# Two joined transformer blocks on one core: boundaries with added squares and idle products, gate columns in quarters, taps on tiles 2 and 3, the first norm among the modulation units

## The chip, the cores and the metric

One core of one Trainium2 chip runs the whole program. The metric is device time in microseconds of one execution. The kernel before took 2717.93, the median of three runs (2711.74 to 2718.31).

## The reference

For 512 tokens of width 1024, in fp32: two layers of a first block, then a second block (attention with chosen keys, window attention, MLP).

```python
def first_block(x, c, w_ada, b_ada, ...):
    c_act = silu(c)
    for l in range(2):
        mod = c_act @ w_ada[l] + b_ada[l]
        sh_mix, sc_mix, gt_mix, sh_mlp, sc_mlp, gt_mlp = split(mod, 6)
        h = rms_norm(x, g_pre_mix[l]) * (1 + sc_mix) + sh_mix
        y = mixer(h, ...)
        x = x + gt_mix * rms_norm(y, g_post_mix[l])
        h = rms_norm(x, g_pre_mlp[l]) * (1 + sc_mlp) + sh_mlp
        f = square(relu(h @ w_ff1[l])) @ w_ff2[l]
        x = x + gt_mlp * rms_norm(f, g_post_mlp[l])

def mixer(h, ...):
    x_m, z, glu_a, glu_b = split(h @ w_in)
    x_c = silu(causal_depthwise_conv(x_m, w_conv_m, b_conv_m))      # 4 taps
    q, k, v = ...                        # per head of 256, from x_c, x_c, x_m
    gates = concat(q, k, v) @ w_gates + b_gates                     # 8 columns: 4 input, 4 forget
    h_m = sigmoid(z) * group_layer_norm(mlstm_chunkwise(q, k, v, gates), 4)
    a = causal_depthwise_conv(glu_a * sigmoid(glu_b), w_dw, b_dw)   # 31 taps
    a = silu(group_layer_norm(a, 8))
    return concat(h_m, a) @ w_out
```

## The kernel before

A tensor of 512 tokens by 1024 features lies in SBUF as 8 tiles of 128 features by 512 tokens. Each weight product is done in split precision: weights and tiles are each a high and a low fp32r part, and a product of 128x128 weights is three matmuls (L1944 to L1946). Weights come in chunks of 512x256, 24 matmuls' worth, through a ring of four: SP loads a chunk (L598), ScalarE writes its high part (L856), POOL its low part (L774). Every engine works its queue in program order; what side work stands between which chunks is written out by hand in each engine's program.

**Start.** SP loads x, c and the four first modulation units (`load_ada` L614, each 1024x512 of `w_ada`). TensorE transposes x, VectorE copies it to X (L1449). `ada_unit` on VectorE multiplies a unit's eight 128x512 pieces by c and adds them up (L1318, L1321); `ada_columns` (L2017) sums over partitions on TensorE.

**A norm.** `norm_stats`: ScalarE squares eight tiles (L886); `norm_sums` on TensorE adds each over its rows with products against one column of ones, 8 a tile (L1990); ScalarE takes the root (L879), VectorE refines it (L1334 to L1341), TensorE spreads it over partitions (L1997). `normalise` then makes each tile: VectorE product (L1355), ScalarE high half (L896), VectorE low half (L1361). Where a residual is added, the added value comes of L1380, X of L1383, and the squares of X follow tile by tile. For the first norm after a product, POOL already adds the squares (`sum_squares`, L783).

**A layer of the first block.** The gated stage: four pair-chunks of `glu_a` and `glu_b` (L1483 makes the gated tile); in layer 0 the rest of the modulation streams in here, one unit a stage p. Then xm, V, Q, K, the gates, z, the heads, the output product, a boundary, the MLP in four groups, a boundary. The 31-tap convolution of a pair of tiles (`long_conv`, L1424 and L1429) is VectorE's; two tiles (6 and 7 before) have a share of their taps scaled by ScalarE (L942, L952) and added by POOL (`taps.add`, L800). `short_conv` is the 4-tap one, `xm_low` (L1491) and `xc_low` (L1497) low parts of the V, Q and K operands. The gates are 8 output rows of one bank (L2091), with transposes of V between (L2075); VectorE adds the bias, centres the values (L1533) and runs the scans; in the z stage it squares the convolved tiles centred (L1561) on means that TensorE forms (L2116). After the last convolution come the modulation's bias and gains (L1682 to L1689), ahead of the boundary.

## Time and profile before

| | us |
|---|---|
| median of three runs | 2717.93 |
| the profiled execution, on the device | 2711.68 |
| its span in the trace | 2709.8 |
| TensorE busy (PE) | 2543.5, 94% |
| VectorE (DVE) | 1281.1, 47% |
| POOL | 1064.7, 39% |
| ScalarE (ACT) | 967.7, 36% |

The span is all that happens between the first and the last instruction; 1.9 us lie around it. Busy time counts matmuls, arithmetic and copies, not waits. The mean granted clock of TensorE was 0.919 of full speed (1.00 is 2.4 GHz, 0.50 is 1.2 GHz).

### The profile page before, as it was taken

Reading aid. Unit: us, or ns where it says so; the run is one execution under the profiler, and the core shown is the slowest. Engines: PE = TensorE matmul, PEld = TensorE weight load, DVE = VectorE, ACT = ScalarE, POOL = GpSimd, SP = SyncE. Lnnn points to the kernel's source line nnn. Section 1 sums busy time; section 2 is a strip of 40 time slices with the busy share of each in tenths; the row PEclk is TensorE's granted clock in tenths of the full one; section 3 lists DMA queues with packets and bytes.
Section 4 is the critical chain, followed back from the end, with each engine's and each line's share of the span. In section 5 each row is a group of like instructions: output and inputs, shape, how many; then the busy total and the mean of one; then the engine's idle time right before and its main releaser. Section 6 shows DMA issues by size and latency. Waiting matters only on the chain.

```text
span 2709.8 us, 29315 instructions
## 1 busy us (share of the span) xinstructions
PE 2543.5 (94%) x10776; PEld 1980.5 (73%) x10776; DVE 1281.1 (47%) x1998; ACT 967.7 (36%) x1530; POOL 1064.7 (39%) x529
## 2 busy tenths in 40 slices
PE   4988899999999999889989999999999999999998
PEld 3776477778888778647777888876776668788887
DVE  4789934754433569973444112124566323312212
ACT  1337553232222333755233223324533322322322
POOL 1348822424434424882242444442421003444443
...
DMA packets 215166, 239.77 MB, mean 88 GB/s; under 512 B 9690, under 2 KB 188698, under 8 KB 215066
## 3 DMA queue, kind: packets, MB, share of 16 engines
...
q8 instruction: 61, 1.00, 0.2%
...
## 4 chain that ended last, share of the span: by engine, by line
PE 81%; DVE 6%; issue 3%; ACT 2%; POOL 2%; DMA 0%; DVEq 0%; SPq 0%; POOLq 0%; ACTq 0%
PE product L1944 21%; PE product L1945 21%; PE product L1946 21%; PE side L1990 3%; PE side L2367 3%; PE product L2389 2%; PE side L2091 2%; PE side L2377 1%; PE side L2174 1%; PE product L2198 1%; PE side L1997 1%; DVE side L1429 1%; POOL slot_f L800 1%; POOL ring_low L774 1%; PE side L2192 1%
## 5 line engine op out<-in xcount | busy, mean ns | idle before, releaser
L774 POOL TENSOR_TENSOR ring_low<-ring_f,ring_high 128x1024 fp32r<-128x1024 f32 (+1 forms) x350 | 838.8, 2402 | 1475.2 <-ACT ring_high L856 1475.2
L1944 PE MATMUL product<-slot_r,ring_high 128*128 128x512 f32 x2792 | 1126.6, 403 | 74.0 <-POOL ring_low L774 29.1
L1945 PE MATMUL product<-slot_r,ring_low 128*128 128x512 f32 x2792 | 1114.5, 399 | 0.0
L1946 PE MATMUL product<-slot_r,ring_high 128*128 128x512 f32 x2792 | 1113.7, 399 | 0.0
L1944 PEld LDWEIGHTS product<-slot_r,ring_high 128*128 128x128 f32 x2792 | 531.1, 190 | 224.6 <-issue 41.7
L856 ACT ACTIVATE ring_high<-ring_f 128x1024 fp32r<-128x1024 f32 (+1 forms) x350 | 367.7, 1053 | 746.8 <-DMA ring_f<-in_w_ff 333.6
L1946 PEld LDWEIGHTS product<-slot_r,ring_high 128*128 128x128 f32 x2792 | 531.4, 190 | 128.6
L1945 PEld LDWEIGHTS product<-slot_r,ring_low 128*128 128x128 f32 x2792 | 532.0, 191 | 123.7 <-issue 0.5
L1398 DVE SCALAR_TENSOR_TENSOR va<-product,sqt 128x512 f32<-128x512 f32 x96 | 66.3, 691 | 391.1 <-ACT sqt L910 391.0
L1429 DVE SCALAR_TENSOR_TENSOR side<-slot_f,cols,side 128x512 f32<-128x512 f32 x332 | 220.7, 747 | 0.0
L1408 DVE TENSOR_TENSOR slot_f<-product,slot_f 128x512 f32<-128x512 f32 x64 | 44.3, 691 | 226.3 <-PE product L1946 226.3
L910 ACT ACTIVATE sqt<-product 128x512 f32<-128x512 f32 x96 | 57.5, 599 | 194.0 <-PE product L1946 194.0
L1990 PEld LDWEIGHTS side<-ones,slot_f 128*128 128x128 f32 x608 | 104.3, 266 | 20.7 <-ACT slot_f L886 12.3
L1990 PE MATMUL side<-ones,slot_f 128*128 128x1 f32 x608 | 104.3, 303 | 11.4 <-ACT slot_f L886 11.1
L1318 DVE SCALAR_TENSOR_TENSOR side<-slot_f,cact,side 128x512 f32<-128x512 f32 x144 | 108.8, 756 | 7.9 <-DMA slot_f<-in_w_ada 2.1
L800 POOL TENSOR_TENSOR slot_f<-slot_f,sqt 128x512 f32<-128x512 f32 x60 | 87.2, 1467 | 26.7 <-ACT sqt L952 26.7
L1408 DVE TENSOR_TENSOR X<-product,X 128x512 f32<-128x512 f32 x32 | 22.1, 692 | 148.2 <-PE product L1946 148.2
L1390 DVE TENSOR_TENSOR slot_r<-va,slot_r 128x512 fp32r<-128x512 f32 x96 | 87.5, 922 | 0.0
L2367 PE MATMUL side<-slot_f 64*128 64x256 f32 (+3 forms) x128 | 80.5, 732 | 5.0 <-DVE slot_f L1842 3.6
L800 POOL TENSOR_TENSOR slot_f<-slot_f,va 128x512 f32<-128x512 f32 x60 | 81.4, 1374 | 3.0 <-ACT va L952 3.0
L886 ACT ACTIVATE slot_f<-X 128x512 f32<-128x512 f32 x56 | 34.5, 628 | 93.1 <-DVE X L1383 43.4
L2389 PEld LDWEIGHTS product<-slot_f 128*128 128x128 f32 x272 | 64.1, 325 | 1.4 <-DVE slot_f L1850 1.2
...
## 6 DMA issues: line engine op xcount, KB each, us to landing
ring_f<-in_w_ff SPq DMA_DIRECT2D x128, 512.0 KB, 3.7
...
```

The source lines that it names most:

```text
L774: pool.tensor_tensor(ring_low[:, s, :, 0:n], ring_f[:, s, :, 0:n], ring_high[:, s, :, 0:n].bitcast(F32), ALU.subtract).then_inc(low_ready. ...
L800: pool.tensor_tensor(tile(SC, t), tile(SC, t), tap[u % 4], ALU.add).then_inc(tap_used.sem, 1)
L856: act.activation(ring_high[:, s, :, 0:n], ring_f[:, s, :, 0:n], ACT.Copy).then_inc(high_ready.sem, 1)
L1318: ins = dve.scalar_tensor_tensor(ada_acc[:] if b and kk == 3 else PM[0][:], ada_raw(slot, b)[:, kk, :], c_col, PM[0][:], ALU.mult, ALU.add)
L1390: dve.tensor_tensor(tile_r(SD, t), va[:, t % 2, :], tile_r(SC, t).bitcast(F32), ALU.subtract).then_inc(fs_ready.sem, 1)
L1429: ins = dve.scalar_tensor_tensor(sum_out, src(t, k, T), wk, sum_in, ALU.mult, ALU.add)
L1944: pe.matmul(out_ap, high, rhs_high, start=start, stop=False)
L1945: pe.matmul(out_ap, low, rhs_high, start=False, stop=False)
L1946: return pe.matmul(out_ap, high, rhs_low, start=False, stop=stop)
L1990: ins = pe.matmul(sums[:, s:s + 1], squares[:, s * P:(s + 1) * P], ones[:, 0:1], start=start and s == 0, stop=stop and s == BLK - 1)
L2367: pe.matmul(PM[u % 2][:, 0:n], q, (AKD if a else BKD)(kv)[b:b + HD, k0:k0 + n], start=True, stop=True).then_inc(qk_2.sem, 1)
L2389: ins = pe.matmul(bank(o)[:, h * HD:(h + 1) * HD], PT[u % 4][:, s * P:(s + 1) * P], VT[0 if a else 1][:, (k0 + s) * P + kv * HD:(k0 + s) * ...
```

## The change

- **Start.** c and unit 0 are loaded first, then x in four pieces, then units 1, 2 and 3, each to buffers of its own. x's first squares come among the units; its high halves of weights are made after them. Tokens' sums of the first norm stand between the unit columns on TensorE.
- **Gated stage of layer 0.** Half of each later unit's load goes out one pair of chunks earlier.
- **Gates.** The product of each head writes rows of its own, at 32 times the head, and the four run for one weight column group each; a second picking product adds and moves the forget rows.
- **Taps.** The tap shares are tiles 2 and 3 instead of 6 and 7 and begin at chunk 11 instead of 21; ScalarE and POOL do them two a chunk through the gated, xm and later stages. The convolution order of VectorE shifts by a pair.
- **Boundaries.** The squares at residual additions are added on POOL, as at the other norms; TensorE has products with the identity and no use (`keep_busy`) while it waits. Bias and gain operations go to places ahead of the boundary, or behind it. POOL's additions stand before three low parts of the next stage.

```diff
 SHARES = NT - SHARED
+TAP_TILE = 2
 TAPS = (CONV_C - 1) * SHARES
-TAPS_FROM = 21
+TAPS_FROM = 11
...
-            sp.dma_start(x_rows, w["x"][0].rearrange("(s p) d -> p s d", p=P)).then_inc(x_loaded.sem, 16)
-            sp.dma_start(c_rows, w["c"][0].rearrange("(t p) -> t p", p=P)).then_inc(x_loaded.sem, 16)
-            for unit in range(ADA_FIRST):
-                load_ada(0, unit_cols(unit), unit)
+            def load_first(unit):
+                for b in range(2):
+                    src = w["w_ada"][0, b * 4 * P:(b + 1) * 4 * P, unit_cols(unit)]
+                    sp.dma_start(ada_raw(FIRST_RAW[unit], b), rows_of(src)).then_inc(first_loaded[unit].sem, 16)
+            sp.dma_start(c_rows, w["c"][0].rearrange("(t p) -> t p", p=P)).then_inc(c_loaded.sem, 16)
+            load_first(0)
+            for s in range(BLK):
+                sp.dma_start(x_rows[:, s, :], w["x"][0, s * P:(s + 1) * P, :]).then_inc(x_loaded.sem, 16)
+            load_first(1)
...
-                        load_ada(l, unit_cols(ADA_FIRST + p), ADA_FIRST + p)
+                        load_ada(l, unit_cols(ADA_FIRST + p), ADA_FIRST + p, halves=(0,))
+                    load_pair(LAYER, I_GLU + 4 * p + 2, w_in, 0, 2 * D + p * CW, load_params if l and p == 0 else None)
+                    if l == 0:
+                        load_ada(l, unit_cols(ADA_FIRST + p), ADA_FIRST + p, halves=(1,))
...
                 taps = Taps()
-                for i in range(I_GATE):
+                early = 2 if l else 0
+                for i in range(early):
+                    low_part(place, LAYER, i)
+                sum_squares(place, 0)
+                for i in range(early, I_GATE):
...
                         taps.add(place, 2)
-                taps.add(place, 26)
+                taps.add(place, 10)
...
                     low_part(place, LAYER, i)
-                    taps.add(place, 4)
+                    taps.add(place, 2)
...
+                sum_squares(place, 1)
+                sum_squares(place, 2)
...
                         low_part(Place(l, g), LAYER, i)
-                sum_squares(place, 3, 1)
+                sum_squares(place, 3)
...
             low_part(place, SECOND, 0)
+            low_part(place, SECOND, 1)
...
-            for i in range(AHEAD):
-                high_part(Place(), LAYER, i)
+            for t in range(NT):
+                wait(act, Place(), xt_done, t + 1)
+                act.activation(X[:, t, :], PB[t % 4][:], ACT.Copy).then_inc(x_ready.sem, 1)
...
                 norm_stats(place, 0, lambda t: X[:, t, :], lambda t: wait(act, place, x_ready, t + 1))
+                if l == 0:
+                    for i in range(AHEAD):
+                        high_part(place, LAYER, i)
                 split_high(place, 0, lambda t: shift[:, t:t + 1])
+                taps = Taps()
...
                         ahead.of(place, I_GLU + 4 * p + t % 2)
+                        if t == 4:
+                            taps.first(place)
+                        if p > 1 and t % 2 == 0:
+                            taps.make(place, 2)
...
                         act.activation(tile(SC, t), bank(o_glub(t))[:], ACT.Sigmoid).then_inc(taken[o_glub(t) % 4].sem, 1)
+                    if p > 1:
+                        taps.make(place, 2)
                     ahead.of(place, I_GLU + 4 * p + 2)
+                    if p > 1:
+                        taps.make(place, 2)
                     ahead.of(place, I_GLU + 4 * p + 3)
+                    if p > 1:
+                        taps.make(place, 2)
...
-                taps = Taps()
...
                     ahead.of(place, I_XM + t)
+                    if t % 2 == 0:
+                        taps.make(place, 2)
...
-                token_rstd(place, m)
+                if place.layer or m:
+                    token_rstd(place, m)
+                else:
+                    wait(dve, place, r_ready, 1)
...
+                def add_bias(a, b):
+                    steps.wait()
+                    steps.did(dve.tensor_tensor(md[:, a:b], md[:, a:b], cols[:, V_BADA + a:V_BADA + b], ALU.add))
+                    steps.wait()
+                def gate_gain(dst, m, g):
+                    steps.did(dve.tensor_tensor(scale[:, dst * NT:(dst + 1) * NT], md[:, m * NT:(m + 1) * NT],
+                                                cols[:, g:g + NT], ALU.mult))
+                def post_mixer():
+                    gate_gain(1, 2, V_GPOSTM)
+                    steps.did(dve.tensor_copy(shift[:, NT:2 * NT], md[:, 3 * NT:4 * NT]))
+                def pre_hidden():
+                    steps.did(dve.scalar_tensor_tensor(scale[:, 2 * NT:3 * NT], md[:, 4 * NT:5 * NT], 1.0,
+                                                       cols[:, V_GPREF:V_GPREF + NT], ALU.add, ALU.mult))
...
+                if l:
+                    add_bias(16, 48)
+                    post_mixer()
...
-                long_conv(place, 2, 0, 14)
+                long_conv(place, 4, 0, 14)
...
                 ada_take()
+                if l == 0:
+                    add_bias(16, 32)
+                    post_mixer()
                 if l:
-                    long_conv(place, 2, 14, 20)
+                    long_conv(place, 4, 14, 20)
...
                 if l:
-                    long_conv(place, 2, 20, 24)
+                    long_conv(place, 4, 20, 24)
...
                 xm_low(4, 5)
+                xm_low(6, 7)
                 short_conv(place, 6)
-                xm_low(6, 7)
                 xc_low(0, 1, 2, 3)
-                long_conv(place, 2, late, late + 3)
+                long_conv(place, 4, late, late + 3)
                 xc_low(4, 5, 6, 7)
-                long_conv(place, 2, late + 3)
-                long_conv(place, 4, 0, 12 if l == 0 else 22)
+                long_conv(place, 4, late + 3)
+                long_conv(place, 6, 0, 12 if l == 0 else 22)
...
                 wait(dve, place, vtr_done, 8)
-                dve.tensor_scalar(gt, PM[0][0:8, :], bgate, None, ALU.add).then_inc(gates_biased.sem, 1)
...
-                steps.did(dve.scalar_tensor_tensor(glf, PM[1][0:HEADS, :], 0.0, gu, ALU.min, ALU.subtract))
+                steps.did(dve.scalar_tensor_tensor(glf, forget_gates, 0.0, gu, ALU.min, ALU.subtract))
...
+                        pre_hidden()
...
                 ada_take()
-                steps.wait()
-                steps.did(dve.tensor_tensor(md[:, 16:48], md[:, 16:48], cols[:, V_BADA + 16:V_BADA + 48], ALU.add))
-                steps.wait()
-                for dst, m, g in ((1, 2, V_GPOSTM), (3, 5, V_GPOSTF)):
-                    steps.did(dve.tensor_tensor(scale[:, dst * NT:(dst + 1) * NT], md[:, m * NT:(m + 1) * NT],
-                                                cols[:, g:g + NT], ALU.mult))
-                steps.did(dve.scalar_tensor_tensor(scale[:, 2 * NT:3 * NT], md[:, 4 * NT:5 * NT], 1.0,
-                                                   cols[:, V_GPREF:V_GPREF + NT], ALU.add, ALU.mult))
-                steps.did(dve.tensor_copy(shift[:, NT:2 * NT], md[:, 3 * NT:4 * NT]))
...
                 normalise(place, 2, 1, lambda t: scale[:, 2 * NT + t:2 * NT + t + 1], lambda t: shift[:, NT + t:NT + t + 1])
+                if l == 0:
+                    add_bias(40, 48)
+                    gate_gain(3, 5, V_GPOSTF)
...
-            def norm_sums(place, m, chain=None):
-                if chain is not None:
-                    wait(pe, place, sq_sums, (NT - 2) * (chain + 1))
+            def keep_busy(side, n):
+                for _ in range(n):
+                    pe.matmul(side[:], ident[:], ones[:, 0:1].to_broadcast([P, T]), start=True, stop=True)
+            def norm_sums(place, m, updates=False, busy=(0, 0), between=None):
+                side = PM[1] if updates else PM[0]
+                if updates:
+                    for t in range(NT - 1):
+                        wait(pe, place, sq_ready, 8 * m + t + 1)
+                        keep_busy(side, 1)
+                    wait(pe, place, sq_ready, 8 * m + NT)
+                    token_sums(PM[3], square(m, NT - 1), True, False)
+                    wait(pe, place, sq_sums, (NT - 2) * (m + 1))
+                    ins = token_sums(PM[3], square(m, 0), False, True)
+                else:
+                    wait(pe, place, sq_sums, (NT - 2) * (m + 1))
                     token_sums(PM[3], square(m, 0), True, False)
-                for t in range(NT) if chain is None else (NT - 1,):
-                    wait(pe, place, sq_ready, 8 * m + t + 1)
-                    ins = token_sums(PM[3], square(m, t), t == 0, t == NT - 1)
+                    wait(pe, place, sq_ready, 8 * m + NT)
+                    ins = token_sums(PM[3], square(m, NT - 1), False, True)
                 ins.then_inc(sq_summed.sem, 1)
+                keep_busy(side, busy[0])
+                if between is not None:
+                    between()
...
             pe.wait_ge(consts.sem, 1)
-            pe.wait_ge(x_loaded.sem, 32)
+            pe.wait_ge(c_loaded.sem, 16)
...
             for t in range(NT):
+                if t == 0:
+                    pe.wait_ge(x_loaded.sem, 16 * BLK)
...
                 ins.then_inc(xt_done.sem, 1)
-            for k in range(ADA_FIRST):
-                ada_columns(Place(), k)
...
                 place = Place(l)
+                if l == 0:
+                    ada_columns(place, 0)
+                    ada_columns(place, 1)
+                    wait(pe, place, x_ready, 5)
...
                 for r, n in ((0, V_BCN + NT), (1, P), (2, P), (3, (CONV_C - 28) * NT)):
-                    ins = pe.transpose(PM[0][:, r * P:r * P + n], rows[0:n, r, :], ident[0:n, 0:n])
+                    ins = pe.transpose(params_bank(l)[:, r * P:r * P + n], rows[0:n, r, :], ident[0:n, 0:n])
                 ins.then_inc(cols_done.sem, 1)
-                norm_sums(place, 0)
+                if l == 0:
+                    norm_sums(place, 0, between=lambda: ada_columns(place, 2))
+                    ada_columns(place, 3)
+                else:
...
-                                n += 1
-                                if a == len(kinds) - 1 and dt == 1 and hd == HEADS - 1:
-                                    ins.then_inc(done.sem, 1)
-                                if n % 3 == 0:
-                                    value_transposes(n // 3 - 1)
+                                ins = pe.matmul(PM[0][32 * hd:32 * hd + 32, :], weights[:, 2 * a + dt, :], src,
+                                                start=kind == 0 and dt == 0, stop=kind == 2 and dt == 1)
+                            if a == len(kinds) - 1 and dt == 1:
+                                ins.then_inc(done.sem, 1)
+                            for _ in range(2 if kind == 2 else 1):
+                                value_transposes(moved)
+                                moved += 1
...
                     else:
-                        wait(pe, place, tap_used, TAPS - SHARES + t - SHARED + 1)
+                        wait(pe, place, cv_ready, conv_count(t))
...
                     ada_columns(place, ADA_GLU + 3)
-                norm_sums(place, 1, 0)
-                norm_sums(place, 2)
+                norm_sums(place, 1, busy=(2, 0))
+                norm_sums(place, 2, True, (2, 3))
...
             mlp_group(Place(LAYERS, FF - 1), SECOND, J_FF, U_FF, 0)
-            norm_sums(place, 2, 1)
+            norm_sums(place, 2, busy=(2, 2))
```

## Rows read from the trace of the kernel before

**Rows 1.** Page: head, and the costliest groups.
```profile
span 2709.8 us, 29315 instructions
...
PE 2543.5 (94%) x10776; PEld 1980.5 (73%) x10776; DVE 1281.1 (47%) x1998; ACT 967.7 (36%) x1530; POOL 1064.7 (39%) x529
...
L774 POOL TENSOR_TENSOR ring_low<-ring_f,ring_high 128x1024 fp32r<-128x1024 f32 (+1 forms) x350 | 838.8, 2402 | 1475.2 <-ACT ring_high L856 1475.2
...
L800 POOL TENSOR_TENSOR slot_f<-slot_f,sqt 128x512 f32<-128x512 f32 x60 | 87.2, 1467 | 26.7 <-ACT sqt L952 26.7
```
**Rows 2.** Who waited for whom, TensorE: us in total, times, longest.
```profile
PE product L1944 <- POOL ring_low L774: 29.1, 7, 8.9
PE side L2017 <- DVE ada_acc L1318: 27.3, 4, 7.7
```
**Rows 3.** Timeline, VectorE 15:54: start, us, what, count [idle before, releaser].
```profile
24.14 0.75 DVE L1321 TENSOR_SCALAR side<-slot_f,cact 128x512 f32<-128x512 f32 x1 [2.06 <-DMA slot_f<-in_w_ada]
...
32.44 0.75 DVE L1321 TENSOR_SCALAR side<-slot_f,cact 128x512 f32<-128x512 f32 x1 [1.89 <-DMA slot_f<-in_w_ada]
```
**Rows 4.** Timeline, TensorE 46:73.
```profile
52.71 13.81 PE L1990 MATMUL side<-ones,slot_f 128*128 128x1 f32 x64
...
72.47 0.77 PE L1944 MATMUL product<-slot_r,ring_high 128*128 128x512 f32 x1 [2.47 <-DVE slot_r L1361]
```
**Rows 5.** Stretches: length, busy PE, PEld, DVE, ACT, POOL, PEclk, DMA, GB/s.
```profile
5.00:10.00 5.00, 1.21 (x6) 1.22 (x7) 0.00 (x0) 0.88 (x1) 0.00 (x0) 1.00 1.03 408
...
540.00:545.00 5.00, 2.08 (x8) 1.78 (x8) 2.80 (x6) 0.53 (x1) 0.00 (x0) 0.50 0.14 50
...
570.00:575.00 5.00, 5.00 (x23) 4.04 (x22) 4.14 (x6) 3.06 (x4) 0.42 (x1) 1.00 0.09 17
```
**Rows 6.** Timeline of three engines, layer 0's gated stage.
```profile
98.21 0.99 SPq L614 DMA_DIRECT2D slot_f<-in_w_ada  x2
...
104.55 0.75 DVE L1321 TENSOR_SCALAR side<-slot_f,cact 128x512 f32<-128x512 f32 x1 [6.10 <-DMA slot_f<-in_w_ada]
...
186.75 0.77 PE L1944 MATMUL product<-slot_r,ring_high 128*128 128x512 f32 x1 [5.50 <-DVE slot_f L1483]
```
**Rows 7.** Timeline, TensorE: gate products, and 64-row scores in the second block.
```profile
279.04 2.74 PE L2091 MATMUL side<-slot_f,ring_f 128*8 128x512 f32 x6
...
1952.75 0.70 PE L2348 MATMUL side<-slot_f 64*128 64x256 f32 x4
```
**Rows 8.** Timeline, VectorE in layer 0, 228:343.
```profile
228.12 1.53 DVE L1424 TENSOR_SCALAR side<-slot_f,cols,small 128x512 f32<-128x512 f32 x2 [2.83 <-issue]
...
295.52 0.74 DVE L1533 TENSOR_SCALAR slot_f<-side,small 8x512 f32<-8x512 f32 x1 [3.67 <-PE product L2075]
...
336.97 1.29 DVE L1561 SCALAR_TENSOR_TENSOR slot_f<-side,slot_f 128x512 f32<-128x512 f32 x2
...
341.94 0.69 DVE L1561 SCALAR_TENSOR_TENSOR slot_f<-side,slot_f 128x512 f32<-128x512 f32 x1 [3.69 <-PE side L2116]
```
**Rows 9.** Timeline, TensorE in the z stage of both layers.
```profile
316.72 0.80 PE L1944 MATMUL product<-slot_r,ring_high 128*128 128x512 f32 x1 [8.87 <-POOL ring_low L774]
...
1220.99 1.88 PE L2116 MATMUL side<-slot_f,ones 128*128 128x512 f32 x4
```
**Rows 10.** Timeline, the mixer's boundary in layer 0, and layer 0's end.
```profile
530.79 1.29 POOL L783 TENSOR_TENSOR slot_f<-slot_f 128x512 f32<-128x512 f32 x1 [5.18 <-ACT slot_f L886]
...
534.47 2.31 DVE L1685 TENSOR_TENSOR scale<-mod,cols 128x8 f32<-128x8 f32 x2
...
540.38 2.08 PE L1997 MATMUL side<-ident,inv_cols 128*128 128x128 f32 x8 [5.83 <-DVE inv_cols L1341]
...
545.15 13.81 PE L1990 MATMUL side<-ones,slot_f 128*128 128x1 f32 x64 [2.70 <-ACT slot_f L886]
...
564.93 0.76 PE L1944 MATMUL product<-slot_r,ring_high 128*128 128x512 f32 x1 [2.47 <-DVE slot_r L1361]
...
940.30 1.35 PE L1997 MATMUL side<-ident,inv_cols 128*128 128x128 f32 x8 [1.42 <-DVE inv_cols L1341]
```

134 lines of the change are left out of this document (86 added, 48 removed).

## The prediction

> **What bounds the kernel now.** I read, in this order, the page's first block, the list of who waited for whom, then the timeline of every stretch where TensorE stood idle for over 0.7 us. TensorE is busy for 94% of the span [rows 1], and nearly all of that is split-precision products, which the change leaves alone. What can move is the 166 us in which it has no work, and the stretches where it is busy with little (sums over squares, gate rows, slow clock). The longest list of waits says where: POOL's low halves of weights, 29.1 us in 7 waits, and the modulation columns at the start, 27.3 us in 4 [rows 2]. In time order the reader should see five kinds of place. (a) The start: the first product begins at 72.47 [rows 4], with VectorE's modulation units waiting for their DMAs [rows 3]. (b) Layer 0's gated stage, where VectorE is the pace and TensorE waits 5.50 us for it [rows 6]. (c) The gate and z stage of both layers, where POOL is late by 8.87 us and VectorE's convolution ends last [rows 8, 9]. (d) The boundaries where a residual is added and the next norm taken: 13.81 us of one-column sums at the slow clock, and short steps one after another [rows 10]. (e) The end, which is short.
>
> **Part 1, the start: -26 us.** Before, one pair of buffers serves all four units: a unit's VectorE work is 6.4 us (24.14 to 32.44 less the wait of 1.89), and with the wait it is 8.3 [rows 3]. Now each has a slot of its own, c is loaded first, and x lies between units 0 and 1. The queue moved 408 GB/s when kept full [rows 5], 5.1 us for 2.1 MB; with the first bytes at about 2.9, unit 0 has landed at 8, x at 13, unit 1 at 18, and units 2 and 3 ahead of need. VectorE then runs three units without a stop: 18.3 + 3 x 6.4 = 37.5, plus 0.8 for the parameter copies. The 13.81 us of input squares [rows 4] go off the path, six of their eight groups replaced by POOL's additions and the rest done while VectorE works. After the last unit come the rstd refinement (0.9), spread (2.1) and unit 3's columns (8 passes, 1.7, from 64 in 13.81), small copies and bias (1.0), and the 2.5 us that the first normalised tile takes [rows 4]: 46.5. That is 26 earlier. The bounds are 22, if the small parameter DMAs ahead of unit 2 or chunk 2 behind unit 4's first half hold things, and 29, if DMA starts sooner. The weight chunks land by 41 and are covered by the wait for unit 3; without that cover each late chunk costs its own landing time.
>
> **Part 2, layer 0's gated stage: -6.** Unit 5's load is issued at 98.21 and VectorE sits idle 6.10 us until 104.55 [rows 6]. Its first half now goes out one chunk pair earlier, its second one stays; the first half's 3.2 us of work (half of 6.4) fall into the wait, and the second half has less to share the queue with: VectorE is some 5.3 earlier. It is busy without a gap from there to the 5.50 us wait at 186.75, so TensorE's restart comes 5.3 earlier, and with a gap that short perhaps without the slow products after it. Against: the taps of tiles 2 and 3 now start here. ScalarE gets two scalings per chunk, POOL two additions of 1.47 each beside a low part of 2.4 [rows 1]: 5.3 of the 5.6 us that TensorE takes per chunk of 24 products (23 or 24 start in 5 us [rows 5], 0.23 apart in the trace). Hidden, but with 0.3 us to spare. Range -2 to -8.
>
> **Part 3, gate columns.** Before: 24 products into 8 columns, 48 passes of 0.45 us (6 in 2.74 with the last one's tail [rows 7]), 21.4 us a layer, and 8 groups of transposes. After: four heads in four column quarters. From above: they run one after another, nothing gained, plus 0.9 for a second picking product. From below: four at once, 21.4 to 5.4. The nearest row is the pair of 64-row products in different row halves: 4 passes of 256 columns, in a line 0.22 each and 0.89 with no tail, end in 0.70 with the last one's tail in it [rows 7], so they overlap in part. I take a factor of two, -8 us of TensorE.
> The Trainium skill (TensorE: Matmul & The Clock Gate, Part 3) states that three column tiles gave 2.38 times, and that weight loads run ahead beside products only where the row group differs, which speaks against four times here, since all rows are used; no row of this trace shows column tiles. By its 2.38 the term would be an estimated -11 instead of -8, and neither changes what ends last in layer 0.
>
> **Part 4, the z stage: layer 0 -13, layer 1 -23.** POOL's additions are spread over chunks from 11 on, instead of a burst of 26 and then 4 a chunk: the waits of 8.87 (one a layer [rows 9]) and of 3.1 at the fifth z chunk (of the 29.1 [rows 2]) go in both layers. In layer 0 VectorE is next. It waited 3.67 for the gates at 295.52 and then ran to 336.97 without a stop, 41.4 us [rows 8]. With the gate stage shorter by 8 the 3.67 go; the low part of tile 6 moves into the 2.83 idle at 228.12 [rows 8], 2.4; and POOL being less busy, operations with two SBUF inputs wait less for it, here 3 to 7 of the 41 plus those before. So VectorE ends some 10 to 13 earlier, at about 325 on the old scale, and TensorE's third mean, at 341.9 before [rows 8], follows at once: -13 (bounds -4 and -18). Layer 1 has most of this convolution done before, so TensorE is the pace: gates -8, POOL's waits -12, slow products after them -1.5, K stage -2.4, second picking product +0.9: -23 at 1220.99 [rows 9] (bounds -12 and -27).
>
> **Part 5, boundaries: -5.8 twice, -2.6, -2.4.** There are four with added squares. Squares come in pairs, the last 8.2 us after the first; 64 one-column passes take 13.81 [rows 10]. POOL's six additions of 1.29 run behind them and end at 9.4; one pass group of 1.0 and it is done at 10.5: -3.3. The clock is at its lower level (0.50) in such a stretch [rows 5], and one-column sums did not raise it in 13.81 us; a dummy product is two passes of 0.45 [rows 7], 0.9 at 2.4 GHz and 1.8 at 1.2. Seven of these fit in 8.2 us only at the higher level; started low, three of them last 5 us, and products did bring the clock up between 565 and 570, where it is at 1.00 from 570 on [rows 5, 10]. The spread then takes 1.35 rather than 2.08 [rows 10]: -0.7. Two dummies outlast the 1.4 us refinement [rows 10] by 0.4 (by 2.2 if slow), three the tile's 2.5 by 0.2. Update part: -3.4 (-1 to -4.5).
> Ahead of the mixer's boundary the bias and gain operations leave the path, in both layers: 5.83 idle becomes 1.8 to 3.6, and two of those took 2.31 for 8 columns beside POOL [rows 10]. With the spread's 0.7, that is -2.3 to -4.8, middle -3.8. Against it, POOL's three low parts of the next stage now stand behind the sums and are still running when the first normalised tile's low half, an operation with two SBUF inputs, wants to go: +1.4 (0 to 2.3). Together -5.8.
> The Trainium skill (SBUF — State Buffer, who interferes with whom) has this as an exclusive lock for a whole instruction between a GpSimd operation and a VectorE one with two SBUF inputs; the 2.31 us row agrees. By that rule applied to all eight low halves the boundary would lose an estimated 7, but POOL has only three parts to do there, so the sum keeps 1.4.
> At the end of a layer the residual's spread came 1.42 after [rows 10], already short, so the dummies there cost 0.4 to 2.2: -2.6 and -2.4. In the second block's middle norm and last norm there are only dummies: +1.0 each (0 to 3.5).
>
> **The sum.** -26 -6 -13 -23 -5.8 -5.8 -2.6 -2.4 +1 +1 = -82.6. The gate columns are inside part 4. Profiled span 2709.8, execution 2711.7: 2629.1. That execution is the fastest of the runs shown, 6 below their median 2717.9; by the median it would be 2635. I say 2632.
>
> **Rivals.** *A, quarters in a line.* Layer 1 loses the 8, layer 0's VectorE waits for the gates about 5 of it: 13 less, 2645. For it: no row shows column tiles; against: the row halves overlap.
> *B, POOL sets the pace.* The additions from chunk 11 on slip, so that low parts come late in the gated and projection stages. The wait that VectorE shows beside POOL [rows 10] may work the other way round: with 0.4 more on each addition a chunk is 6.1 us against 5.6, and 0.5 on 19 chunks, twice, is 19 us: 2651. Against it: POOL is busy for 39% of the span, and the ring holds four chunks.
> *C, slower than before.* The same mechanism, with ScalarE in it: its scalings wait for POOL's additions, its high halves stand behind them in order, POOL's low halves behind those. It decides the sign once a chunk from 11 to 29 takes over 5.6 + 83/38 = 7.8 us in both layers; at 8.2, 2730. Against it: ScalarE is busy for 36% of the span [rows 1], and there are four tap buffers between the two.
> *D, the start is held by something else* (the PE's order, small DMAs, the slow clock), and gives 14 instead of 26: 2644.
> *E, all goes well*: locks gone, clock up, four quarters at once: 2612.
> *F, dummies at 1.2 GHz everywhere*, so that each of the boundaries loses its gain: 2652.
>
> **Chances.** Forecast (2620 to 2640) 0.40; A 0.14; B 0.10; C 0.04; D 0.12; E 0.11; F 0.06; the change does in part not what it says, ending within 0.3% of before, 0.03. Range for 8 in 10: the unknown bounds summed in squares give about 17 on each side, and A, B, D and F reach to 2655: 2606 to 2660. A measurement here can tell some 0.3% from no change. Faster by over 0.3%: 0.93; within: 0.03; slower: 0.04.
>
> **What would show it.** First product at 46 or so, three modulation units back to back (part 1). Restart in layer 0's stage within 1 us of the need (part 2). Starts of the four quarter products closer than 0.89 us (part 3); no wait for POOL's low halves after the gates, VectorE's convolution ending ahead of a single idle stretch of TensorE in layer 0, none in layer 1 (part 4). Two short sum groups instead of 64 passes, done 10.5 us after the first square, PEclk at 1.0 by the first product, one VectorE low half over 1.5 us (part 5). The prediction is wrong if ring waits appear between chunks 11 and 29, or if VectorE's modulation units still wait for DMAs.

## The result, and the profile after

The changed kernel takes 2626.77 us (median of four, 2624.44 to 2628.85) against 2717.32 for the kernel before (median of four): a ratio of 0.9682, 95% interval 0.9668 to 0.9695, or 91 us less by the medians. The profiled execution is the second fastest of the four, 2624.85, 87 below the profiled one of before. The forecast was 2632, with 8 chances in 10 for 2606 to 2660. Page head and the list of who waited for whom (TensorE; us in total, times, longest) of the changed kernel, where the lines of the weight products are now L2042 to L2044:

```profile
span 2623.1 us, 29172 instructions
...
PE 2502.1 (95%) x10670; PEld 1926.1 (73%) x10670; DVE 1261.5 (48%) x1995; ACT 971.4 (37%) x1538; POOL 1106.6 (42%) x559
```
```profile
PE side L2248 <- DVE slot_f L1633: 14.3, 2, 7.2
...
PE side L2238 <- DVE slot_f L1662: 7.6, 1, 7.6
...
PE product L2042 <- POOL ring_low L804: 4.3, 2, 4.0
```

Against [rows 2] POOL's late low halves fell from 29.1 us to 4.3, and the modulation columns from 27.3 to one wait of 5.7. In their place stand two waits of 7.2 (one a layer) for VectorE's gate bias (L1633), and one of 7.6 for its convolution, in layer 0. TensorE is busy for 41 us less, and idle for 45 less.

Every kernel here has the same 2792 high-part products in the same order, so the n-th of them is a milestone. The start of the same product in both traces, and what lies between:

| up to | before | after | moved | this part | forecast |
|---|---|---|---|---|---|
| first product | 72.47 | 50.59 | -21.9 | -21.9 | -26 |
| restart in layer 0's gated stage | 186.75 | 164.94 | -21.8 | +0.1 | -6 |
| end of layer 0's z stage | 353.40 | 318.20 | -35.2 | -13.4 | -13 |
| last part of layer 0's output product | 507.97 | 471.74 | -36.2 | -1.0 | 0 |
| mixer's boundary, layer 0 | 564.93 | 522.29 | -42.6 | -6.4 | -5.8 |
| layer 0's end | 964.11 | 919.09 | -45.0 | -2.4 | -2.6 |
| z stage of layer 1 | 1276.95 | 1205.26 | -71.7 | -26.7 | -23 |
| heads of layer 1 | 1347.02 | 1272.21 | -74.8 | -3.1 | 0 |
| mixer's boundary, layer 1 | 1444.11 | 1363.42 | -80.7 | -5.9 | -5.8 |
| layer 1's end | 1833.83 | 1749.42 | -84.4 | -3.7 | -2.4 |
| end of the span | 2709.8 | 2623.1 | -86.7 | -2.3 | +2 |

**The start.** Timeline of VectorE, POOL and TensorE (start us, us, what, count [idle before, releaser]):

```profile
9.72 0.75 DVE L1377 TENSOR_SCALAR side<-slot_f,cact 128x512 f32<-128x512 f32 x1 [6.91 <-DMA slot_f<-in_w_ada]
...
20.37 0.75 DVE L1377 TENSOR_SCALAR side<-slot_f,cact 128x512 f32<-128x512 f32 x1 [4.30 <-DMA slot_f<-in_w_ada]
...
27.42 0.75 DVE L1377 TENSOR_SCALAR side<-slot_f,cact 128x512 f32<-128x512 f32 x1 [0.63 <-DMA slot_f<-in_w_ada]
...
45.68 2.34 POOL L804 TENSOR_TENSOR ring_low<-ring_f,ring_high 128x1024 fp32r<-128x1024 f32 x1 [5.44 <-ACT ring_high L893]
...
45.90 2.13 DVE L1538 SCALAR_TENSOR_TENSOR scale<-mod,cols 128x8 f32<-128x8 f32 x1
...
50.59 0.76 PE L2042 MATMUL product<-slot_r,ring_high 128*128 128x512 f32 x1 [5.36 <-DVE slot_r L1420]
```

VectorE starts unit 1 at 20.37 and unit 2 at 27.42, as they land: with x, 8.4 MB since the first bytes at about 2.9, 342 GB/s on average. The rate was not that all along. In three stretches of 4 us (length, busy PE, PEld, DVE, ACT, POOL, PEclk, DMA share, GB/s):

```profile
14.00:18.00 4.00, 3.23 (x15) 3.23 (x16) 2.00 (x3) 1.56 (x3) 0.00 (x0) 1.00 1.05 387
18.00:22.00 4.00, 3.13 (x27) 3.04 (x25) 1.56 (x3) 3.74 (x8) 0.00 (x0) 1.00 1.07 311
22.00:26.00 4.00, 0.00 (x0) 0.00 (x0) 3.79 (x6) 3.98 (x8) 3.46 (x3) 0.93 1.04 384
```

The dip to 311 has as high a DMA share as its neighbours; in it run the small parameter loads that SP issues between units 1 and 2, some 400 packets of 512 bytes. Later an operation on 8 columns takes 2.13 us while POOL works on a low part.

**The gated stage.** VectorE, POOL, TensorE:

```profile
83.79 2.34 DVE L1374 SCALAR_TENSOR_TENSOR side<-slot_f,cact,side 128x512 f32<-128x512 f32 x3 [3.78 <-DMA slot_f<-in_w_ada]
...
113.15 2.46 DVE L1488 SCALAR_TENSOR_TENSOR side<-slot_f,cols 128x512 f32<-128x512 f32 x2
...
113.31 3.45 POOL L830 TENSOR_TENSOR slot_f<-slot_f,va 128x512 f32<-128x512 f32 x2
...
164.94 0.77 PE L2042 MATMUL product<-slot_r,ring_high 128*128 128x512 f32 x1 [6.63 <-DVE slot_f L1574]
```

The wait of 5.50 [rows 6] is still there, as 6.63. Unit 5's second half lands after VectorE has used the first, and an operation that took 1.42 us for its pair before takes 2.46 beside POOL's tap additions, once for each of two pairs.

**Gates and z stage, layer 0**, TensorE:

```profile
241.38 1.07 PE L2213 MATMUL side<-slot_f,ring_f 128*32 128x512 f32 x8
...
265.44 1.87 PE L2248 MATMUL side<-slot_f,ident_sums 128*4 128x512 f32 x2 [7.22 <-DVE slot_f L1633]
...
302.71 3.75 PE L2238 MATMUL side<-slot_f,ones 128*128 128x512 f32 x4 [7.60 <-DVE slot_f L1662]
```

Eight passes into four quarters take 1.07 us, last tail and all, where six into 8 columns took 2.74 [rows 7]. Behind them TensorE waits twice for VectorE.

**A boundary**, layer 0's mixer (TensorE, and VectorE's refinement). The sums begin 8.5 us after the first square is done (at 503.5) and end in 2.43 (64 passes in 13.81 [rows 10]). The two idle products at 514.35 (four passes) run until 518.1; the spread waits for them and starts at 517.91, 2.1 us past the refinement's end:

```profile
503.56 7.01 PE L2102 MATMUL side<-ones,ident 128*128 128x512 f32 x12 [2.70 <-ACT slot_f L923]
...
512.06 2.43 PE L2088 MATMUL side<-ones,slot_f 128*128 128x1 f32 x16
...
514.35 3.76 PE L2102 MATMUL side<-ones,ident 128*128 128x512 f32 x4
...
515.69 0.16 DVE L1397 SCALAR_TENSOR_TENSOR inv_cols<-side,inv_cols 128x4 f32<-128x4 f32 x1
...
517.91 1.92 PE L2095 MATMUL side<-ident,inv_cols 128*128 128x128 f32 x8
```

### The profile page after: what moved, and what is told of

It reads as the page before. It is cut to its first block, busy times and chain, and to the rows that moved or that the text cites. A ratio compares the mean times of both kernels' runs of the same rounds, so it can differ in the third digit from the quotient of the medians.

```text
span 2623.1 us, 29172 instructions
## 1 busy us (share of the span) xinstructions
PE 2502.1 (95%) x10670; PEld 1926.1 (73%) x10670; DVE 1261.5 (48%) x1995; ACT 971.4 (37%) x1538; POOL 1106.6 (42%) x559
## 4 chain that ended last, share of the span: by engine, by line
PE 81%; DVE 11%; ACT 1%; issue 1%; POOL 1%; DVEq 0%; POOLq 0%; ACTq 0%
PE product L2042 22%; PE product L2044 22%; PE product L2043 22%; DVE side L1488 5%; PE side L2490 3%; PE product L2512 2%; PE side L2500 1%; PE side L2297 1%; PE product L2321 1%; PE side L2088 1%; PE side L2095 1%; PE side L2102 1%; DVE slot_r L1589 1%; PE side L2315 1%; POOL slot_f L813 1%
## 5 line engine op out<-in xcount | busy, mean ns | idle before, releaser
L2042 PE MATMUL product<-slot_r,ring_high 128*128 128x512 f32 x2792 | 1120.1, 401 | 39.1 <-DVE slot_r L1420 9.3
L2044 PE MATMUL product<-slot_r,ring_high 128*128 128x512 f32 x2792 | 1107.1, 397 | 0.0
L2042 PEld LDWEIGHTS product<-slot_r,ring_high 128*128 128x128 f32 x2792 | 527.4, 189 | 190.4 <-issue 35.3
L2044 PEld LDWEIGHTS product<-slot_r,ring_high 128*128 128x128 f32 x2792 | 527.1, 189 | 126.3
L813 POOL TENSOR_TENSOR slot_f<-slot_f 128x512 f32<-128x512 f32 x66 | 84.5, 1280 | 95.9 <-ACT slot_f L923 89.4
L830 POOL TENSOR_TENSOR slot_f<-slot_f,va 128x512 f32<-128x512 f32 x60 | 88.5, 1494 | 2.7 <-ACT va L989 2.4
L830 POOL TENSOR_TENSOR slot_f<-slot_f,sqt 128x512 f32<-128x512 f32 x60 | 81.5, 1379 | 16.1 <-ACT sqt L989 16.1
L2102 PE MATMUL side<-ones,ident 128*128 128x512 f32 x130 | 74.7, 712 | 12.9 <-ACT slot_f L923 12.9
```

The costliest lines, as they stand in the source:

```text
L813: pool.tensor_tensor(square(m, 0), square(m, 0), square(m, t), ALU.add).then_inc(sq_sums.sem, 1)
L830: pool.tensor_tensor(tile(SC, t), tile(SC, t), tap[u % 4], ALU.add).then_inc(tap_used.sem, 1)
L2042: pe.matmul(out_ap, high, rhs_high, start=start, stop=False)
L2044: return pe.matmul(out_ap, high, rhs_low, start=False, stop=stop)
L2102: pe.matmul(side[:], ident[:], ones[:, 0:1].to_broadcast([P, T]), start=True, stop=True)
```

## Experiments

Each is the changed kernel with the edit shown. Medians are of four runs; ratios are to the kernel before on the same chip, where the changed kernel has 0.9682 (0.9668 to 0.9695). A per cent of the ratio is 27 us, so the intervals are some 4 to 7 us to either side. Where a number of microseconds is said to come of the medians, it is the run's median less 2626.77; the kernel before took 2712.7 to 2714.6 on the chips of these runs and 2717.3 on that of the result, so such a number can be off by some 3 to 5 us, and the ratios go before it. Single places are compared by the milestones. They agree to 0.5 us at the first product where an edit leaves it alone. Further on they step without any edit there. Between the milestones at 318 and 425 us of the changed kernel its own profiled execution had the clock at 1.00 nearly throughout, and eight of the eleven others lost up to 6 us there with no more than 0.6 us more of idle time: with x first (e9), the first 12 us of that stretch had a mean granted clock of 0.80, and 5.9 us are lost in all. In the second block five of the profiled executions lost 3.5 to 4.4 us in the same way. So behind layer 0's z stage a difference of under some 6 us between two milestones tells little, unless the place itself shows the wait.

No run takes back the added squares of the boundaries alone, or the start's buffers alone; what these gave rests on the milestones. The expectations call the runs by the names in the headings.

### Gates in line (e2): 2641.08, 0.9733 (0.9709 to 0.9757)

```diff
-ins = pe.matmul(PM[0][32 * hd:32 * hd + 32, :], weights[:, 2 * a + dt, :], src, ...)
+ins = pe.matmul(PM[0][0:8, :], weights[:, 2 * a + dt, 8 * hd:8 * hd + 8], src, ...)
-pe.matmul(forget_gates, gate_pick[:, HEADS:2 * HEADS], gate_parts, ...)
+pe.matmul(forget_gates, gate_pick[0:8, HEADS:2 * HEADS], gate_parts[0:8, :], ...)
```

> The changed kernel with all gate products in the same 8 rows, as before, and the picking products taking them from there. Theory 1, the four quarters run at once: 48 passes in line take 21.4 us where the quarters take 6.4, so the gate stage grows by 15 us in each layer; behind it TensorE waited 7.2 us for VectorE's bias, which goes, so layer 1 loses 8 us and layer 0, where VectorE sets the end of the z stage and was 13 us behind the gates, only 2 or 3: 2637 in all. Theory 2, the gain of the gate stage came from its transposes and order and not from the quarters: the stage grows by under 4 us, and the kernel stays within 2 us of the changed one.

```profile
241.94 3.60 PE L2213 MATMUL side<-slot_f,ring_f 128*8 128x512 f32 x8
```
```profile
267.70 0.74 DVE L1633 TENSOR_SCALAR slot_f<-side,small 8x512 f32<-8x512 f32 x1 [2.42 <-PE product L2197]
...
269.71 8.50 DVE L1643 TENSOR_SCALAR slot_f<-slot_f,small 128x256 f32<-128x256 f32 x16
```

Eight passes take 3.60 us: the quarters run at once, 3.4 times as fast. The stage grew by 14.9 us in layer 0 and 14.4 in layer 1, and 9.0 and 8.9 came back right behind it from the wait for the bias. Layer 1 lost 5.5 where 8 were expected. Layer 0 was to lose 2 or 3 and lost 6 to 9, by the milestone: VectorE started the bias 3 us later, and then its 16 centring operations (L1643) took 8.50 us instead of 4.29. Theory 1 holds for the mechanism; where the rest came from is the subject of the runs below.

### Taps as before (e6): 2664.69, 0.9813 (0.9797 to 0.9830)

```diff
-TAP_TILE = 2
-TAPS_FROM = 11
+TAP_TILE = 6
+TAPS_FROM = 21
-                taps.add(place, 10)
+                taps.add(place, 26)
...
-                    taps.add(place, 2)
+                    taps.add(place, 4)
...
-                long_conv(place, 4, 0, 14)
+                long_conv(place, 2, 0, 14)
```
(and ScalarE's taps at the places before)

> The changed kernel with the taps of tiles 6 and 7 as before: they start at the xm stage, POOL adds 26 of them in a burst at the gates and then 4 a chunk, VectorE convolves the pairs in the order before. Theory 1, the burst is what made POOL's low halves late: the first z chunk's low half comes 9 to 14 us late, of which TensorE's 7 us wait for VectorE hides a half; layer 1 loses 8 to 12 us, layer 0, where VectorE is the bound, 0 to 4, less the 2.2 us that VectorE lost to the earlier taps in the gated stage: 2633 to 2641. Theory 2, the waits for POOL went with the shorter gate stage and the order of ScalarE's work: no wait for POOL over 3 us comes back, and the kernel is within 3 us of the changed one or faster.

Who TensorE waited for, and its timeline:

```profile
PE product L2031 <- POOL ring_low L804: 50.4, 8, 11.2
```
```profile
267.07 0.80 PE L2031 MATMUL product<-slot_r,ring_high 128*128 128x512 f32 x1 [11.22 <-POOL ring_low L804]
...
291.02 0.79 PE L2031 MATMUL product<-slot_r,ring_high 128*128 128x512 f32 x1 [9.10 <-POOL ring_low L804]
```

38 us by the medians and 36 by the ratios and by the traces, where 6 to 14 were expected: waits of 11.2 and 9.1 for POOL behind layer 0's gates and in its z stage, 50.4 us in all where before had 29.1 [rows 2]. Layer 0 lost 7.6 us up to its mixer's boundary and layer 1 another 25. The burst is the same 26 additions, while the gate stage that covers a part of it is 15 us shorter. That this is why the waits grew is argued, not shown by a run of its own. Spreading the taps was worth 36 us in the changed kernel, though only 29 us of such waits stood in the old trace. The edit takes back the order of the convolution and of ScalarE's scalings with the taps; the runs don't part the three.

### The start: x first (e9) 2627.97, 0.9682 (0.9666 to 0.9698); chunks before unit 4 (e7) 2627.76, 0.9681 (0.9665 to 0.9697)

```diff
-load_first(0)
 for s in range(BLK):
     sp.dma_start(x_rows[:, s, :], ...)
+load_first(0)
```

> The changed kernel with x loaded ahead of the first modulation unit instead of between units 0 and 1. Unit 2 lands at 27.4 in the changed kernel (8.4 MB in some 24.5 us, 342 GB/s). Theory 1, the sum of the bytes up to unit 2 sets the start, and VectorE's idle times ahead of it take up the order: the first product stays within 0.5 us of 50.6. Theory 2, the prediction's picture, in which VectorE runs from unit 0 on without a stop: unit 0 lands some 5 us later and the first product comes 5 us later.

```profile
14.75 0.75 DVE L1377 TENSOR_SCALAR side<-slot_f,cact 128x512 f32<-128x512 f32 x1 [11.94 <-DMA slot_f<-in_w_ada]
```
```profile
50.85 0.77 PE L2042 MATMUL product<-slot_r,ring_high 128*128 128x512 f32 x1 [5.46 <-DVE slot_r L1420]
```

VectorE starts 5.0 us later, TensorE's first product 0.3. That is theory 1's number, and the reason is the one it gives: VectorE's idle times ahead of unit 2 took up the order. With x first VectorE runs from 14.75 on without a stop and begins unit 2 at 27.59; in the changed kernel it waits 4.30 and 0.63 us and begins unit 2 at 27.42. Both bounds lie in the same place here, so this run can't tell what a faster queue alone would give.

```diff
 load_pair(LAYER, I_GLU + 4 * p, ...)
-if l == 0:
+if l == 0 and p:
     load_ada(..., halves=(0,))
 load_pair(LAYER, I_GLU + 4 * p + 2, ...)
 if l == 0:
-    load_ada(..., halves=(1,))
+    load_ada(..., halves=(1,) if p else (0, 1))
```

> The changed kernel with the third and fourth chunk of weights loaded ahead of unit 4 instead of behind its first half, which SP issues only at 37.64. There the low half of the third chunk ran on POOL from 45.68 to 48.0 and VectorE's 8-column gain operation took 2.13 us beside it. Theory 1, that is the 2 us by which the start was late behind the refinement: POOL is done before, and the first product comes 1.9 us earlier (48.7), the kernel with it. Theory 2, the gain operation waits for something else, or the earlier chunks push unit 3 back on the queue: the first product comes at the same time or later.

```profile
45.99 0.17 DVE L1538 SCALAR_TENSOR_TENSOR scale<-mod,cols 128x8 f32<-128x8 f32 x1
```

The same operation takes 0.17 us with POOL done, and the first product comes at 48.71, 1.9 earlier. At the gated stage's restart 1.2 of the 1.9 were left, eight high-part products on 0.6, and the median did not move. Theory 1 holds for the place, and not for the end.

### Whole units earlier (e3): 2624.26, 0.9673 (0.9654 to 0.9691)

```diff
-load_ada(..., halves=(0,))
+load_ada(..., halves=(0, 1) if p else (0,))
 load_pair(LAYER, I_GLU + 4 * p + 2, ...)
-if l == 0:
+if l == 0 and p == 0:
     load_ada(..., halves=(1,))
```

> The changed kernel with both halves of modulation units 5, 6 and 7 loaded one pair of chunks earlier, not the first half alone. In the changed kernel unit 5's second half lands after VectorE has used the first, an idle time of 3.78 us, and VectorE is busy without a gap from there to TensorE's wait of 6.63 us. Theory 1, VectorE's chain through the gated stage sets the restart: the idle time goes and the restart, and all that follows in layer 0 and behind it, comes 3.7 us earlier: 3.7 below the changed kernel (2623). Theory 2, the queue is what is short: unit and chunk share the queue, the chunk behind the unit comes late, and the gain is under 1 us or a loss.

```profile
160.53 0.47 PE L2042 MATMUL product<-slot_r,ring_high 128*128 128x512 f32 x1 [2.62 <-DVE slot_f L1574]
```

VectorE's idle time of 3.78 is gone and the restart 4.4 us earlier; 3.6 are left at the last product. The gain at the restart is shown by the wait itself; the gain of the whole is not, since the intervals of the two ratios overlap (2.5 us by the medians). The queue was not short: it was the place of the second half in it.

### Bias early (e4) 2641.19, 0.9727 (0.9705 to 0.9749); filling an idle time (e5) 2629.40, 0.9686 (0.9660 to 0.9711)

```diff
-long_conv(place, 6, 0, 12 if l == 0 else 22)
+long_conv(place, 6, 0, 12)
...
-long_conv(place, 6, 12 if l == 0 else 22)
+long_conv(place, 6, 12)
```

> The changed kernel with ten of the taps of tiles 6 and 7 in layer 1 put behind the gates on VectorE, so that layer 1 has the split of layer 0. Theory 1, VectorE comes to the gate bias too late because of the convolution queued ahead of it (TensorE's picking product waited 7.13 us there): the bias comes 13 us earlier, the wait goes, of which some 2 us come back at the first convolution means, which stand behind the same convolution: layer 1 5 us shorter, 2622 in all. Theory 2, VectorE's sum of work sets the end there: the wait moves whole to the means, 0.

```diff
-late = 14 if l == 0 else 24
+late = 18 if l == 0 else 24
...
 short_conv(place, 0)
+if l == 0: long_conv(place, 4, 14, 18)
 short_conv(place, 2)
```

> The changed kernel with four taps of tiles 4 and 5 (8 operations of 0.66 us, 5.3 us) in layer 0 moved into VectorE's idle time of 5.71 us in the xm stage. Theory 1, in layer 0 VectorE's work from the gated stage to the convolution means sets the end, so all of its idle time counts: the wait of TensorE at the means falls from 7.60 to 2.3 and layer 0 ends 5 us earlier: 2622. Theory 2, the short convolution behind the moved taps comes late and holds the V and Q stages instead: no gain, or up to 3 us more.

Both were to give 5 us; the first lost 14 (12 by the ratios) and the second gained nothing. What they have in common stands in one row each: the stretch in which VectorE centres the values (16 operations of 128x256, in place) in four kernels. Columns: length, busy PE, PEld, DVE, ACT, POOL, PEclk, DMA share, GB/s. The changed kernel:

```profile
265.50:269.80 4.30, 4.30 (x6) 1.04 (x7) 4.29 (x16) 2.35 (x3) 0.00 (x0) 0.50 0.00 0
```

before:

```profile
296.60:306.10 9.50, 9.50 (x39) 6.83 (x38) 9.46 (x18) 7.24 (x10) 6.23 (x4) 1.00 0.35 104
```

with the idle time filled:

```profile
262.00:272.50 10.50, 10.50 (x45) 8.10 (x44) 10.46 (x17) 9.16 (x12) 7.52 (x5) 1.00 0.18 53
```

with the bias early, layer 1:

```profile
1113.70:1126.40 12.70, 12.70 (x51) 8.83 (x50) 12.70 (x17) 11.29 (x15) 9.97 (x6) 1.00 0.28 83
```

With POOL idle the 16 operations take 4.29 us; beside 6.2, 7.5 and 10.0 us of POOL's work they take about 9.5, 10.5 and 12.7, longer by 5.2, 6.2 and 8.4, so some 0.83 us for each of POOL's. The other engines are at work in the longer stretches as well. Cutting the stretch of the kernel before where POOL stops tells them apart:

```profile
296.60:302.85 6.25, 6.25 (x25) 4.22 (x24) 6.21 (x5) 4.01 (x7) 6.23 (x4) 1.00 0.31 87
302.85:306.10 3.25, 3.25 (x16) 2.62 (x15) 3.25 (x14) 3.22 (x4) 0.00 (x0) 1.00 0.41 136
```

Four of the 16 fall into the first part and last 1.34 to 2.48 us each, one for each operation of POOL; twelve fall into the second, start 0.27 apart and last 0.34, with TensorE and ScalarE busy almost without a gap. With the idle time filled it is the same: five last 1.3 to 2.5 us beside POOL, eleven 0.34 without it. So it is POOL, and an operation of VectorE that meets one of POOL's lasts as long as that one.

In the changed kernel POOL stands still there. VectorE's bias is late, so TensorE's picking product is; ScalarE waits for that product in its queue, ahead of its next high half; and POOL waits for the high half (timelines of ScalarE and POOL):

```profile
267.40 0.59 ACT L1089 ACTIVATE slot_f<-side 4x512 f32<-4x512 f32 x1 [6.83 <-PE side L2248]
...
271.70 2.40 POOL L804 TENSOR_TENSOR ring_low<-ring_f,ring_high 128x1024 fp32r<-128x1024 f32 x1 [7.77 <-ACT ring_high L893]
```

VectorE's lateness buys VectorE its undisturbed centring. Take the lateness away and POOL is at work. With the bias early there was a second cause: the ten taps moved behind the gates came on top, and TensorE waited for the means, 10.29 us in layer 1.

```profile
1158.46 3.75 PE L2238 MATMUL side<-slot_f,ones 128*128 128x512 f32 x4 [10.29 <-DVE slot_f L1662]
```

I had expected 2 us there, because I had put the means' need 8 us too late. Filling the idle time brought VectorE 4.7 us earlier to the bias (259.89 for 264.63) and let it end its convolution 1.2 later (303.05 for 301.87).

How VectorE meets POOL also changes from run to run. In layer 0 of the run with the bias early the program is that of the changed kernel. Yet four low parts ahead of the bias (`xc_low`) took 4.41 us, where they took 7.75 in the changed kernel (at 220.43):

```profile
219.45 4.41 DVE L1589 TENSOR_TENSOR slot_r<-slot_f,slot_r 128x512 fp32r<-128x512 f32 x4
```

VectorE came to the bias 4.2 us earlier, 3.3 of them by this; TensorE still waited 3.42 there, the centring took 5.25 and the convolution ended 3.0 earlier. So 3 us in layer 0's z stage can come of no edit.

The Trainium skill (SBUF — State Buffer, who interferes with whom) gives the shared port pair to whichever starts first, a GpSimd operation or a VectorE one that has two SBUF inputs (beside a GpSimd one that reads SBUF) or runs in a two-port performance mode, for the whole instruction. The centring has one SBUF input, so it would fall under the rule's second half; that it runs in such a mode no run here shows directly. That a centring operation is held for the whole of one operation of POOL, these rows show. The prediction had used only the first half.

### Centring on ScalarE (e10): 2619.08, 0.9648 (0.9631 to 0.9664); and all together (e11): 2607.80, 0.9611 (0.9591 to 0.9631)

```diff
-dve.tensor_scalar(v, v, v_sums[:, at:at + 1], None, ALU.add)        # 16, behind the bias
+long_conv(place, 6, *((10, 14) if l == 0 else (15, 19)))
...
+act.activation(v, v, ACT.Identity, bias=v_sums[:, at:at + 1])       # 4 in each of z chunks 1 to 4
...
-long_conv(place, 6, 0, 12 if l == 0 else 22)
+long_conv(place, 6, 0, 10 if l == 0 else 15)
```
(and the filled idle time)

> The changed kernel with the centring of the values on ScalarE in the z stage (16 activations, spread over four chunks) instead of VectorE behind the gate bias; VectorE has the four taps of the run e5_fill in its idle time, comes to the gate bias earlier (10 and 15 taps of tiles 6 and 7 ahead of it), and fills the wait for the forget gate's logarithm with four more. Theory 1, what ate the gains of e4 and e5 was the centring: its 16 operations took 4.29 us in the changed kernel only because POOL stood idle, held by TensorE's wait for VectorE, and 10.5 to 12.8 us once VectorE came earlier and met POOL at work. Off VectorE, the time that it comes earlier is kept: layer 0's convolution means 8 to 11 us earlier (TensorE's wait of 7.6 us gone), layer 1's gates 6 to 7: 2609 to 2613. Theory 2, the gains were eaten by the length of VectorE's convolution and TensorE's own order: under 4 us gained, or ScalarE's extra work makes high halves late.

```profile
294.87 3.75 PE L2242 MATMUL side<-slot_f,ones 128*128 128x512 f32 x4 [8.01 <-DVE slot_f L1666]
```

Both waits for the bias are gone. The means of layer 0 come 7.8 us earlier, at 294.87, and layer 1 gains another 7 to 8 up to product 1224. The median gained 8 (9 by the ratios, whose intervals don't overlap) of the expected 14 to 18. The wait of 8.01 shows what is missing: TensorE is now also 8 us earlier there, so layer 0's z stage still ends with VectorE. Of its 7.8, some 3.3 are again those four low parts, which took 4.41 us for 7.75, so what the edit gave in layer 0 may be no more than 4.5. By layer 0's end 2.7 are left, since slower products fell into it: between the milestones at 318 and 330 us of the changed kernel the mean granted clock was 0.80 for 1.00, with no idle time in either.

> The kernel of e10_centre_on_act with the load order of e3_units_whole (whole units one pair of chunks earlier) and of e7_chunks_before_unit (third and fourth chunk ahead of unit 4). Theory 1, the gated stage still follows VectorE: 3.7 us more than e10, and of the start's 1.9 us none more, because VectorE's chain through the gated stage takes it up: 2605 to 2610. Theory 2, with layer 0's z stage no longer held by VectorE these 3.7 us show in full and the start's too: 2603 to 2607.

```profile
285.90 3.47 PE L2242 MATMUL side<-slot_f,ones 128*128 128x512 f32 x4 [8.03 <-DVE slot_f L1666]
```

With the loads of the two other runs the means come another 9.0 us earlier and the kernel ends 11 us below the last: 2607.80, 19 less than the changed kernel and 106 less than the kernel before, and the fastest of all. The start's 1.9 us and the units' 4.4 add up at the restart (6.5 earlier), which is theory 2's mechanism; the time itself lies in theory 1's range and 0.8 above theory 2's, and the interval of some 5 us to either side holds both.

### Idle products: none (e1) 2631.72, 0.9692 (0.9666 to 0.9718); none before the spread (e8) 2630.31, 0.9685 (0.9669 to 0.9701)

```diff
 def keep_busy(side, n):
-    for _ in range(n):
+    for _ in range(0):
```

> The changed kernel without any idle product (the waits for the squares stay). In the changed kernel's trace the two products put ahead of a spread end after the refinement at five of eight places and hold the spread for 2.0, 1.75, 1.1, 1.8 and 1.8 us, 8.5 in all. Theory 1, the idle products pay through the clock: without them the granted clock falls in every boundary, each spread takes 2.08 us instead of 1.05 and the first products after it run slow for some us, so 1.0 + 1.5 at each of eight spreads is lost and 8.5 won back: the kernel is 5 to 12 us slower than the changed one (2632 to 2639). Theory 2, they only cost: it is about 8 us faster (2619).

```profile
512.55 3.55 PE L2088 MATMUL side<-ones,slot_f 128*128 128x1 f32 x16 [10.98 <-ACT slot_f L923]
...
517.52 2.08 PE L2095 MATMUL side<-ident,inv_cols 128*128 128x128 f32 x8 [1.42 <-DVE inv_cols L1397]
...
522.07 0.77 PE L2042 MATMUL product<-slot_r,ring_high 128*128 128x512 f32 x1 [2.47 <-DVE slot_r L1420]
```

```diff
-norm_sums(place, 2, True, (2, 3))
+norm_sums(place, 2, True, (0, 3))
```
(and so at the other six calls)

> The changed kernel with the idle products beside the squares and behind the spread, but without the two between the sums and the spread. Theory 1, these two are only late work: 8.5 us of waits ahead of spreads go and the clock stays as it is: 8 us faster than the changed kernel (2619). Theory 2, they are what keeps the clock up for the spread and the products behind it: the waits go but spreads take 2.08 us and the first products are slow: within 2 us of the changed kernel.

Without any idle product the sums take 3.55 us for 2.43, the spread 2.08 for 1.92, and the first product of layer 0's MLP comes at 522.07 against 522.29: here the idle products win nothing, because the pair ahead of the spread gives back what the clock gains. At layer 0's end they win 1.7 us, and there they hold the clock (the same stretch of the changed kernel, 900:905, has 1.00):

```profile
900.00:905.00 5.00, 1.15 (x6) 0.69 (x4) 4.67 (x8) 1.44 (x3) 1.27 (x1) 0.50 0.00 0
```

By the medians the two kernels are 5 and 3.5 us slower than the changed one, by the ratios 2.7 and 0.8, with overlapping intervals. So the 8.5 us of waits ahead of the spreads are real in the trace, but taking them away brought nothing; whether the pair itself pays stays open. For the idle products as a whole the milestones give 2.8 us up to the end of layer 1. The ratios allow anything from a loss of some 5 us to a gain of some 10, so that they pay at all is not shown.

## Why the prediction came true, point by point

**Start: the mechanism right, the size 4 too high.** VectorE's chain after unit 2, and the order of the steps behind it, went as worked out. Two terms were mis-sized. Units and x came at 342 GB/s on average, not the 408 of the row I took (a stretch in which x alone was under way): 384 to 387 where units are under way, and 311 in the 4 us in which the parameters' small packets are among them, so the last three units began at 20.37 instead of 18.3 and, with 0.63 more of waiting, ended 2.5 us late. And "small copies and bias, 1.0" held an operation with two SBUF inputs, which met POOL's low part: 2.13 for 0.17. The prediction had this very effect at the boundaries and did not look for it here. The prediction's own sign of being wrong, modulation units that still wait for DMAs, is there: 4.30 and 0.63 us, and 3.78 at unit 5. Its other one, ring waits between chunks 11 and 29, is not.

**Gated stage: wrong.** The step that failed is "its second one stays; the first half's work falls into the wait". It did, but the second half then landed 3.78 us after it was wanted, so 2.1 of the 5.3 were gained. These went to the taps: the prediction asked whether POOL could keep up with them (it could) and not what they do to VectorE, where two pairs of operations each grew by 1.0 to 1.1. Whole units earlier brought the restart 4.4 us earlier, for the 3.7 of idle time expected.

**Gate columns: the factor.** I took 2, from two row halves; the runs show 3.4 (3.60 to 1.07 us for eight passes). The Trainium skill (TensorE: Matmul & The Clock Gate, Part 3) has 2.38 for three tiles; no run here has three, and that all rows are used, which was to speak against four, did not show as a cost. The stage gained 14.9 us: its 48 passes take 6.4 us, near the lower bound of 5.4. Layer 0 was not to feel it. It did: with the gates in a line (e2) its z stage ends 6.2 us later.

**z stage: right sizes, partly for other reasons.** Layer 0: -13.4 for -13. The forecast's terms were 3.67 us of waiting for the gates, 2.4 for a low part in an idle time, and 3 to 7 us less waiting for POOL. From the restart to the bias VectorE gained 9.1 us, and its idle time there fell by 8.8 (18.0 to 9.2), the 3.67 among them; its low parts beside POOL took no less in sum. Then came the centring in 4.29 us for 9.46 (the stretches above), a gain of 5.2 that no sentence of the prediction named. So the term "less waiting for POOL" came true in size, at an operation with one SBUF input that it did not mean, and for a reason that it did not have.

Layer 1: -26.7 for -23. The gates gave 14.8 for 8. POOL's waits went (8.88 and 3.06 us), with the slow products behind them 14.6, for 13.5. The stages ahead of the gates gave 7.0, for 2.4. Against them stood the wait of 7.13 for VectorE's bias, which the prediction did not have: with the quarters overlapping nearly in full, VectorE was late in layer 1 as well, and 9.6 us went there, with the second picking product (0.9 in the forecast). Here errors of the prediction cancelled.

**Boundaries: right.** -6.4 and -5.9 for -5.8; -2.4 and -3.7 for -2.6 and -2.4. Sums began at 8.5 us and ended at 10.9 (forecast 10.5). The cost of idle products at the slow clock was foreseen at up to 2.2 us and was 2.1 here. The 1.4 us for POOL's low parts beside the first normalised tile did not come: POOL had ended its three at 519.9, as VectorE began, and the low half took 0.75. The spread's 2.1 us of lateness came in their place.

**Not forecast:** 3.1 us among layer 1's heads. There is no wait there in either trace; the products are slower in the kernel before, timeline of TensorE:

```profile
1338.72 0.63 PE L1946 MATMUL product<-slot_r,ring_high 128*128 128x512 f32 x1
```

where the same product of the changed kernel took 0.39 (1266.27). It is a stretch at the lower granted clock that the later kernel does not have at this place. The mean granted clock of the part is 0.951 before and 1.00 after. In the second block, norms with idle products were to cost 1 each and the part gained 2.3.

**The total is in part luck.** The parts sum to -86.7 for a forecast of -82.6. Start and gated stage fell short by 10.2 us. The heads of layer 1 and the end, for which there was no forecast of a gain, and the z stage of layer 1 gave 11.1 more than said. That the total is within 5 us of the forecast says less for it than the parts do.

**The rivals.** A (quarters in a line) is refuted by the gate run; B and C (POOL or ScalarE as the pace) by 4.3 us of waits in all for low halves, 4.0 of them in the second block. D was a matter of 4 us, not of 12. Of E the quarters came true, but VectorE took 7 us of them in each layer. F (idle products at the lower clock everywhere, so that each boundary loses its gain) did not come: they were slow at layer 0's mixer boundary and not at its end, and all four boundaries gained.
